# The output projection of a hybrid decoder layer as seven half products (Strassen's scheme) instead of eight

## The chip, the cores and the metric

The kernel runs on one core of one Trainium2 chip. The metric is device time in microseconds (us) of one execution. The engines are TensorE (PE; its weight loads are shown apart as PEld), VectorE (DVE), ScalarE (ACT), GpSimd (POOL) and SyncE (SP). SP issues nearly all DMAs here, in the order of its program, and each engine works through its own program in order and waits on semaphores.

## The reference

One layer on 1024 tokens of width 2048. A combined input projection feeds eight HGRN2 heads and four GLA heads, whose readouts are joined to y (1024 x 2048); then

```python
y = jnp.concatenate([y_h, y_g], axis=-1) @ w_out[i]
h = h + y.astype(dtype)

e = rms_norm(p[i] @ ple_proj[i], ple_norm_w[i])
gate = jax.nn.sigmoid(rms_norm(h, ple_gate_norm_w[i]) @ ple_gate_w[i] + ple_gate_b[i])
h = h + (gate * e).astype(dtype)
return rms_norm(h, final_norm_w)
```

The change is in the first of these lines, a product of a 2048 x 2048 weight matrix with the 2048 x 1024 matrix of y.

## The kernel before

All data is feature-major: a tile is 128 features by 512 tokens, and the 1024 tokens are two halves, h = 0 and h = 1. Every large product works with a split of both operands into a high part (rounded to fp32r) and a low part (the rest): three matmuls of 128 x 128 by 128 x 512 for each pair, low weight by high activation and so on (`passes`, L523 to L525). The activations of a stage lie in `act_hi` and `act_lo`, 16 tiles of 128 x 512 each. Writing them is a *fill*: `fill_high` on ACT (a cast to fp32r), then `fill_low` on DVE (source minus high part).

The weights come in *slabs*: 2048 x 128 of a weight matrix, 1 MB, as two halves `w_raw[0]`, `w_raw[1]` of 512 KB. For slab g SP loads the halves (`load_slab`, L371) as soon as the low halves of slab g-1 have been made; ACT casts them to `w_hi` when slab g-2 has been multiplied (`split_weights`, L778); DVE makes `w_lo` (`low_weights`, L1188). A slab takes 16 x 3 = 48 matmuls into one PSUM bank, `acc[0]` for even and `acc[1]` for odd slabs, and PE may start one only when the bank's last result has been taken out (`acc_free`).

The stages are, in order: the product of p (32 tiles), the input projection of half 0 (56 slabs) with the recurrences of its heads hung between the matmuls, the same for half 1, the output projection of half 0 and then of half 1 (16 slabs each), the gate projection of the two halves (16 slabs each), the final norm. The recurrence of a head is placed at fixed places between the matmuls of the next head's slabs (`hooks`): `k_transpose` and `state_update` in the first slab, seven levels (L588) in the second and third, `readout` and `o_transpose` later. The last head's hooks lie in the first slabs of the output projection.

In the output projection DVE takes a finished bank out (`h_begin`, L1565: h = acc + x, with the x tile loaded by SP into `xt_sb`), ACT squares it (L1047), DVE adds the square to a row sum (L1570). In the output projection of half 1, the tiles e of the p product, stored in HBM at the start, are loaded again, squared by ACT and summed by DVE. The readouts y of each head are stored to HBM (`y_scratch`, L380), and loaded before the stage that needs them (`load_y`, L384: four transfers of 1 MB). GpSimd does eight squares at the start of the kernel (L517) and nothing after it.

Of the kernel before, what the change touches and what calls it, by code (L numbers as in the profile page):

```python
# [38 lines left out]
P = 128  # L39
# [22 lines left out]
SLABS = E_SLABS + HALVES * (I_SLABS + 2 * KT)  # L62
# [7 lines left out]
def s_out(h):  # L70
    return E_SLABS + HALVES * I_SLABS + h * KT


def s_gate(h):
    return s_out(HALVES) + h * KT
# [67 lines left out]
def build(nc, x_feat, p, slabs, w_glr, w2, vec, lb_rows, masks, restart, ident_d, out, e_scratch, y_scratch):  # L143
    with ExitStack() as ctx:
# [91 lines left out]
        e_back = [unit(18), unit(21)]  # L236
        e_sqr = unit(20)
# [44 lines left out]
        ROWS_X, ROWS_H, ROWS_E, ROWS_F = (1, 2), (3, 6), (4, 5), (7, 8)  # L282
# [15 lines left out]
        act_free = sem("act_free")  # L298
        g_arg = sem("g_arg")
# [50 lines left out]
        def stage_end(a):  # L350

            return t_of((s_in, s_out, s_gate)[a // 2](a % 2 + 1) - 1)
# [8 lines left out]
        def _(sp):  # L361
            def load_slab(g, half=0):

                if isinstance(g, int):
                    stage = sum(g >= start for start in (s_in(1), s_out(0), s_out(1), s_gate(0), s_gate(1)))
                    at = g - (0, I_SLABS, I_SLABS, I_SLABS + KT, I_SLABS + KT, I_SLABS + 2 * KT)[stage]
                else:
                    at = g - half * I_SLABS
                for j in range(2):
                    sp.wait_ge(w_lo_ready, g * 2 + (j + 1))  # L370
                    sp.dma_start(w_raw[j][:, :], slabs[bass.ds(at, 1), j, :, :].rearrange("o p n -> (o p) n")  # L371
                                 ).then_inc(raw_loaded[j], 16)
# [10 lines left out]
            def load_y(h, q):  # L383
                sp.dma_start((feat, work)[h][:, 4 * q:4 * q + 4, :], y_scratch[h, 4 * q:4 * q + 4].rearrange("k p n -> p k n")  # L384
# [26 lines left out]
            for h in range(HALVES):  # L411
                base = s_in(h)
                if h:
# [4 lines left out]
                    sp.wait_ge(y_stored, h * Y_STORES * 16 + 16)  # L418
                    for q in range(4):
                        load_y(0, q)  # L420
# [3 lines left out]
                with sp.Fori(1, NH) as n:  # L424
                    for j in range(2, 6):
                        load_slab(n * SLABS_H + (base + j), h)
                    store_y(h, n + (h * HEADS - 1), n - 1, 1)
                for s in range(NH * SLABS_H + 2, NH * SLABS_H + 7):
                    load_slab(base + s)
# [1400 lines left out]
```

## Time and profile before

| | |
|---|---|
| median of 3 runs | 2258.35 us (2257.3 to 2260.07) |
| profiled execution, its own time | 2257.98 us |
| its span in the profile | 2255.9 us |
| PE busy | 2228.4 us, 99% of the span |
| PE weight loads, DVE, ACT, POOL busy | 82%, 65%, 44%, 0% |
| mean granted TensorE clock | 0.994 |

The time of the profiled execution is 2.1 us above its span, the start and end that the span does not hold. Busy times overlap between engines. A matmul's row shows its whole passage through the engine, so rows of PE overlap; the distance between starts is what one costs.

### The profile page before, as it was taken

To read this page: it belongs to the slowest core of one execution; us is meant where nothing else is said; L and a number is where in the kernel's file an instruction comes from. 1 tells how busy PE (TensorE), PEld (TensorE's weight loads), DVE (VectorE), ACT (ScalarE), POOL (GpSimd) and SP (SyncE) were. 2 spreads that over 40 slices of the span, in tenths; PEclk is the share of its full clock that TensorE was granted. 3 is DMA by queue.
4 is the path that set the end of the run, shared out by engine and by line. 5 is a ranking of instruction groups with operands and counts; after the bars stand their busy time and mean duration, and the time that the engine had idled before them with its cause. 6 is when DMAs were issued, how large, how long until landed. Compare 5 with 4: busy or idle time off the path is not lost.

```text
span 2255.9 us, 30769 instructions
## 1 busy us (share of the span) xinstructions
PE 2228.4 (99%) x10574; PEld 1857.8 (82%) x10574; DVE 1467.7 (65%) x2885; ACT 996.6 (44%) x1695; POOL 10.2 (0%) x12
## 2 busy tenths in 40 slices
PE   8999999999999999999999999999999999999996
PEld 7888888888888888888888888888888888887885
DVE  7567777775566666767666555566336448768875
ACT  6455544544333444444444333343224336446443
POOL 1000000000000000000000000000000000000000
PEclk9999999999999999999999999999999999999998
DMA  8622222222222224232222322222634553332442
GB/s 288 205 80 80 97 84 92 79 82 96 86 92 84 84 75 164 79 98 83 93 79 80 98 85 93 84 94 92 220 117 154 168 180 113 129 127 106 159 160 102
DMA packets 88438, 257.26 MB, mean 114 GB/s; under 512 B 9232, under 2 KB 9488, under 8 KB 88368
## 3 DMA queue, kind: packets, MB, share of 16 engines
q1 hardware_dynamic: 88368, 256.35, 33.9%
q8 instruction: 41, 0.67, 0.1%
q14 instruction: 29, 0.24, 0.0%
HBM read 231.15 MB, written 25.17 MB: 114 GB/s over the span
## 4 chain that ended last, share of the span: by engine, by line
PE 95%; DVE 2%; ACT 1%; DMA 1%; issue 0%; SPq 0%; DVEq 0%; ACTq 0%
PE acc L523 28%; PE acc L524 28%; PE acc L525 28%; PE lv L588 3%; PE so L597 1%; PE so L600 1%; PE so L577 1%; PE ms L566 1%; DMA w_raw<-in_slabs 1%; DVE sq_sum L1519 1%; DVE act_lo L1207 0%; PE tr L612 0%; PE tr L554 0%; PE tr L562 0%; PE ms L619 0%
## 5 line engine op out<-in xcount | busy, mean ns | idle before, releaser
L523 PE MATMUL acc<-act_hi,w_lo 128*128 128x512 f32 x2880 | 1154.5, 401 | 2.1 <-DVE act_lo L1207 1.4
L525 PE MATMUL acc<-act_hi,w_hi 128*128 128x512 f32 x2880 | 1124.1, 390 | 0.0
L524 PE MATMUL acc<-act_lo,w_hi 128*128 128x512 f32 x2880 | 1123.8, 390 | 0.0
L523 PEld LDWEIGHTS acc<-act_hi,w_lo 128*128 128x128 f32 x2880 | 542.4, 188 | 115.6 <-issue 9.7
L525 PEld LDWEIGHTS acc<-act_hi,w_hi 128*128 128x128 f32 x2880 | 541.1, 188 | 114.6
L524 PEld LDWEIGHTS acc<-act_lo,w_hi 128*128 128x128 f32 x2880 | 542.4, 188 | 104.6 <-issue 2.0
L778 ACT CAST w_hi<-w_raw 128x1024 fp32r<-128x1024 f32 x356 | 357.8, 1047 | 513.7 <-PE acc L525 477.2
L1188 DVE TENSOR_TENSOR w_lo<-w_raw,w_hi 128x1024 fp32r<-128x1024 f32 x356 | 420.3, 1220 | 81.6 <-ACT w_hi L778 81.4
L842 ACT ACTIVATE work<-work 128x512 f32<-128x512 f32 x120 | 75.6, 630 | 163.4 <-DVE work L1254 162.7
L792 ACT ACTIVATE work<-work 128x512 f32<-128x512 f32 x95 | 60.1, 632 | 140.2 <-DVE work L1234 140.2
L1268 DVE COPY_PREDICATED work<-mask_sb,lv 128x256 f32<-128x256 uint8 x168 | 88.6, 528 | 7.2
L588 PEld LDWEIGHTS lv<-work 128*128 128x128 f32 x480 | 71.9, 190 | 9.4
L1260 DVE TENSOR_TENSOR work<-work 128x256 f32<-128x256 f32 x120 | 50.9, 424 | 38.7 <-ACT work L842 38.7
L588 PE MATMUL lv<-work 128*128 128x128 f32 x480 | 72.6, 274 | 0.0
L786 ACT ACTIVATE work<-work 128x512 f32<-128x512 f32 x104 | 65.8, 633 | 3.3
L788 ACT ACTIVATE work<-work 128x512 f32<-128x512 f32 x104 | 65.8, 633 | 3.3
L1172 DVE MEMSET vec_dummy<- 128x1 f32 x209 | 12.3, 59 | 78.4 <-PE lv L588 74.8
L1053 ACT ACTIVATE work<-work 128x512 f32<-128x512 f32 x32 | 20.0, 624 | 87.7 <-DMA work<-e_scratch 85.6
L1565 DVE TENSOR_TENSOR feat<-acc,state_h 128x512 f32<-128x512 f32 (+1 forms) x16 | 11.0, 686 | 70.0 <-PE acc L525 64.2
L1239 DVE SCALAR_TENSOR_TENSOR work<-acc,work 128x512 f32<-128x512 f32 x48 | 33.2, 692 | 33.8 <-ACT work L792 33.8
L1254 DVE TENSOR_TENSOR work<-work 128x256 f32<-128x256 f32 x120 | 50.4, 420 | 0.0
L1253 DVE TENSOR_TENSOR work<-work 128x256 f32<-128x256 f32 x120 | 50.3, 420 | 0.0
(246 smaller groups left out, 1758.5 us busy)
## 6 DMA issues: line engine op xcount, KB each, us to landing
w_raw<-in_slabs SPq DMA_DIRECT2D x356, 512.0 KB, 4.1
work<-e_scratch SPq DMA_DIRECT2D x64, 256.0 KB, 4.6
feat<-in_x_feat SPq DMA_DIRECT2D x8, 1024.0 KB, 12.1
e_scratch<-work SPq DMA_DIRECT2D x32, 256.0 KB, 5.8
state_h<-in_x_feat SPq DMA_DIRECT2D x32, 256.0 KB, 2.6
y_scratch<-work SPq DMA_DIRECT2D x16, 256.0 KB, 2.0
y_scratch<-work SPq DMA_DIRECT2D x8, 512.0 KB, 2.8
feat<-y_scratch SPq DMA_DIRECT2D x4, 1024.0 KB, 9.2
```

The source lines that it names most:

```text
L523: nc.tensor.matmul(ps, lhs_lo, rhs_hi, start=start, stop=False)
L524: nc.tensor.matmul(ps, lhs_hi, rhs_lo, start=False, stop=False)
L525: return nc.tensor.matmul(ps, lhs_hi, rhs_hi, start=False, stop=stop)
L588: last = nc.tensor.matmul(scores[:, :, c * half:(c + 1) * half], x_lv[l % 3][:, c * C:(c + 1) * C], queries[:, :, c * half:(c + 1) * half] ...
L778: nc.scalar.copy(w_hi[par][:, j, :], w_raw[j][:, :]).then_inc(w_hi_ready, 1)
L786: st.mark(A(t1, t1, ACT.Exp, scale=-1.0))
L788: A(t1, t1, ACT.Ln, bias=1.0).then_inc(sp_ready, 1)
L792: A(t2, t2, ACT.Exp).then_inc(sig_ready, 1)
L842: A(x_lv[l % 3], x_lv[l % 3], ACT.Exp).then_inc(lv_exp, 1)
L1188: v.tensor_tensor(w_lo[par][:, j, :], w_raw[j][:, :], w_hi[par][:, j, :].bitcast(F32), ALU.subtract).then_inc(w_lo_ready, 1)
L1260: st.mark(v.tensor_tensor(keys, keys, lower_tokens(k_t, s), ALU.mult))
L1268: v.copy_predicated(upper_tokens(attn, s), mask_sb[:, l, :].rearrange("p (b n s) -> p b n s", b=2, s=s), lv_ps[l % 2][:, 0:TH // 2].rearra ...
```

## The change

y is cut into four blocks of 1024 features by 512 tokens, B11 and B21 of half 0, B12 and B22 of half 1, and w_out into four blocks of 1024 x 1024. The four blocks of the result are made from seven products of a 1024 x 1024 with a 1024 x 512 matrix, in place of eight. Four of the weight matrices are sums of blocks (in the order of the products P5, P6, P7, P3), three are blocks (P1, P2, P4); four of the activations are sums: T1 = B12 - B11, T3 = B22 - B12, T2 = T3 + B11, T4 = T2 - B21 (the signs are those of the code).

*Slabs.* An output slab now holds 8 x 128 weights for each of two tiles: its half j goes to `acc[j]` with 8 x 3 matmuls (`out_parts`). There are 28 slabs: n = 0 to 7 are P1 and P2 in turn, 8 to 15 P5 and P6 in turn, 16 to 19 P3, 20 to 27 P7 and P4 in turn. Both halves of the tokens are finished in one stage, and the gate stage follows.

*Sums of weights.* During the eight HGRN heads of half 1, SP loads each head 2 MB of blocks of w_out into `feat` (`load_blocks`), GpSimd makes four sums of 128 x 1024 (`block_sums`), and SP stores 2 MB to `w_sums` in HBM (`store_sums`).

*Sums of y.* T1 is made by GpSimd in `feat` after the HGRN heads of half 1 (4 MB loaded, 2 MB stored). T3, T2 and T4 are made by GpSimd during output slabs 5 to 11. The last head's y is stored in SP's place for n = 5, then come four loads of 1 MB, and in n = 6 the rows shown below.

*Fills.* Six fills of 8 tiles lie in the output projection (`FILLS_AT`), in the programs of ACT and DVE ahead of the taking out of that slab's banks: T1 at n = 7 for slab 8, T2 at 8 for slab 9, B22 at 15 for slab 16, T3 at 17 for slab 20, T4 at 20 for slab 21, the first half of the gate stage's at 27. T1 comes through four buffers of one tile; B22, T3 and T4 through three, each loaded again once `fill_low` has read it.

```diff
+def out_slab(n):
+    if n < 8:
+        return (P1, P2)[n % 2], n // 2
+    if n < 16:
+        return (P5, P6)[n % 2], (n - 8) // 2
+    if n < 20:
+        return P3, n - 16
+    return (P7, P4)[n % 2], (n - 20) // 2
...
+        FILLS_AT = {7: 10, 8: 11, 15: 12, 17: 13, 20: 14, OUT_SLABS - 1: 4}
...
+            for n in range(OUT_SLABS):
+                for j in range(2):
+                    if n in (2, 4, 6):
+                        load_x_tile(n + j)
+                    if 14 <= n < 18:
+                        load_x_tile(8 + 2 * (n - 14) + j)
+                    if 18 <= n < 26:
+                        load_x_tile(16 + 2 * (n - 18) + j)
...
+                if n == 7:
+                    for k in range(4, HK):
+                        load_t1(k)
...
+                for a, first, rest in ((12, 13, 15), (13, 16, 17), (14, 18, 20)):
+                    for k in range(HK):
+                        if n == (first if k < 3 else rest):
+                            load_t(a, k)
...
+                load_slab(S_OUT + n + 3)
...
+            def block_sums(c):
+                a11, a12, a21, a22 = (feat[:, 2 * u:2 * u + 2, :].rearrange("p k n -> p (k n)") for u in range(4))
+                pool.wait_ge(sum_loaded, c * 64 + 64)
+                g.tensor_tensor(a22, a21, a22, ALU.add).then_inc(sums_done, 1)
+                pool.wait_ge(sums_done, c * 4 + 1)
+                g.tensor_tensor(a21, a11, a21, ALU.subtract).then_inc(sums_done, 1)
...
+                for j in range(2):
+                    pe.wait_ge(acc_free[j], OUT_PAIR + n + 1)
+                    pe.wait_ge(w_hi_ready, g * 2 + (j + 1))
+                    pe.wait_ge(w_lo_ready, g * 2 + (j + 3))
+                    for k in range(HK):
...
+            for n in range(5, OUT_SLABS):
+                low_weights(S_OUT + n + 1, (n + 1) % 2)
+                if n == 21:
+                    row_factors(ROWS_E[0], r_e[0], e_sum[0])
+                if n == OUT_SLABS - 1:
+                    row_factors(ROWS_E[1], r_e[1], e_sum[1])
...
+                first = {5: 4, 7: 6}.get(n, 2 * n - 22 if 15 <= n < 27 else None)
+                if first is not None:
+                    for q in (first, first + 1):
+                        x_part(q)
+                if n in FILLS_AT:
+                    for k in range(HK):
+                        fill_low(FILLS_AT[n], k)
+                if n < OUT_SLABS - 1:
+                    for j in range(2):
+                        out_part(n, j)
+                        out_end(n, j)
+                        if 9 <= n < 25:
+                            e_add(2 * (n - 9) + j)
```

`x_part` adds the x tile, `out_part` adds a finished bank (P2, P3, P4: one addition; P6 and P7: two; P1 and P5 are copied out by ACT), `out_end` adds a square to the row sum. In the first output slabs, ACT and DVE do the last six tiles of y's fill later than before, and DVE takes out P2's first bank behind `next_level(R, 2)` and two `x_part`.

Three places show what stands in a row. The first is SP in the output projection at n = 6, from the loading of slab 8 (its first row) to that of slab 9: x tiles, four tiles of T1 (w2_sb, glr_t and two of work), three of B21, then twice a 1 MB load of B11 behind a wait for GpSimd and a 1 MB store of T3, then slab 9, and only then the last four tiles of T1.

```order
L472 DMA w_raw0<-w_sums 128x1024 [waits w_lo_ready]
L472 DMA w_raw1<-w_sums 128x1024 [waits w_lo_ready]
L563 DMA state_h<-in_x_feat 128x512 [waits xt_used] x2
...
L632 DMA work<-y_scratch 128x4x512 [waits t3_done]
L634 DMA t_sums<-work 128x4x512
L632 DMA work<-y_scratch 128x4x512 [waits t3_done]
L634 DMA t_sums<-work 128x4x512
L472 DMA w_raw0<-w_sums 128x1024 [waits w_lo_ready]
L472 DMA w_raw1<-w_sums 128x1024 [waits w_lo_ready]
L575 DMA w2_sb<-t_sums 128x512 [waits act_lo_ready]
L575 DMA glr_t<-t_sums 128x512 [waits act_lo_ready]
L575 DMA work<-t_sums 128x512 [waits act_lo_ready] x2
```

Before, the same engine had between two slabs of the output projection one x tile, and at one place the four loads of y of half 1.

```order
L371 DMA w_raw0<-in_slabs 128x1024 [waits w_lo_ready]
L371 DMA w_raw1<-in_slabs 128x1024 [waits w_lo_ready]
L384 DMA work<-y_scratch 128x4x512 [waits y_stored]
L384 DMA work<-y_scratch 128x4x512 x3
L443 DMA state_h<-in_x_feat 128x512 [waits acc_free1]
L371 DMA w_raw0<-in_slabs 128x1024 [waits w_lo_ready]
```

The second place is DVE in the output projection at n = 15: low weights of slab 16, two x parts, the eight tiles of B22's fill, and behind them the taking out of slab 15's banks (L1826).

```order
L1436 TENSOR_TENSOR w_lo<-w_raw,w_hi 128x1024 x2
L1816 TENSOR_TENSOR work<-work,state_h 128x512 x2
L1452 TENSOR_TENSOR act_lo<-work,act_hi 128x512 x8
L1826 TENSOR_TENSOR feat<-feat,acc 128x512
L1828 TENSOR_TENSOR work<-work,feat 128x512
L1850 TENSOR_TENSOR state_g<-state_g,work 128x512
```

Before, DVE had for a slab of the output projection of half 0 these rows, with the taking out first.

```order
L1565 TENSOR_TENSOR feat<-acc,state_h 128x512
L1188 TENSOR_TENSOR w_lo<-w_raw,w_hi 128x1024 x2
L1570 TENSOR_TENSOR sq_sum<-sq_sum,work 128x512
```

So the fill moved ahead of the release of a bank, and the same holds at n = 7, 17, 20 and 27. The third place is GpSimd in the HGRN heads of half 1, where nothing stood before:

```order
L699 TENSOR_TENSOR feat<-feat 128x1024 [waits sum_loaded]
L701 TENSOR_TENSOR feat<-feat 128x1024 [waits sums_done]
L703 TENSOR_TENSOR feat<-feat 128x1024 [waits sums_done]
L705 TENSOR_TENSOR feat<-feat 128x1024 [waits sums_done]
```

Each of the four waits for the one ahead; DVE's and PE's programs in these heads did not change.

## Rows read from the trace of the kernel before

**Rows 1.** The page, part 1: busy us, share of the span, instructions.
```profile
PE 2228.4 (99%) x10574; PEld 1857.8 (82%) x10574; DVE 1467.7 (65%) x2885; ACT 996.6 (44%) x1695; POOL 10.2 (0%) x12
```
**Rows 2.** Waits of PE: us in total, times, longest.
```profile
PE lv L636 <- DVE sq_sum L1519: 4.4, 1, 4.4
```
**Rows 3.** Timeline in the output projection: start us, us, engine line.
```profile
1680.33 0.39 PE L525 MATMUL acc<-act_hi,w_hi 128*128 128x512 f32 x1
...
1683.05 0.39 PE L525 MATMUL acc<-act_hi,w_hi 128*128 128x512 f32 x1
```
**Rows 4.** Timelines of DVE and ACT in the output projection of half 0.
```profile
1544.21 0.42 DVE L1254 TENSOR_TENSOR x_lv<-work 128x256 f32<-128x256 f32 x1
...
1556.04 2.01 ACT L778 CAST w_hi<-w_raw 128x1024 fp32r<-128x1024 f32 x2 [7.48 <-PE acc L525]
...
1604.00 2.00 ACT L778 CAST w_hi<-w_raw 128x1024 fp32r<-128x1024 f32 x2 [8.35 <-PE acc L525]
...
1605.08 2.36 DVE L1188 TENSOR_TENSOR w_lo<-w_raw,w_hi 128x1024 fp32r<-128x1024 f32 x2 [0.26 <-ACT w_hi L778]
...
1614.88 2.00 ACT L778 CAST w_hi<-w_raw 128x1024 fp32r<-128x1024 f32 x2 [8.35 <-PE acc L525]
```
**Rows 5.** Timeline of SP, then one row of ACT, around y's loads.
```profile
1587.09 0.43 SPq L380 DMA_DIRECT2D y_scratch<-work  x1
...
1606.34 1.47 SPq L371 DMA_DIRECT2D w_raw<-in_slabs  x2
1607.85 4.26 SPq L384 DMA_DIRECT2D work<-y_scratch  x4
...
1617.22 1.46 SPq L371 DMA_DIRECT2D w_raw<-in_slabs  x2
...
1626.19 1.05 ACT L778 CAST w_hi<-w_raw 128x1024 fp32r<-128x1024 f32 x1 [8.78 <-DMA w_raw<-in_slabs]
```
**Rows 6.** Windows: width, busy us of each engine, clock, DMA share, GB/s.
```profile
1619.00:1622.00 3.00, 3.00 (x15) 2.49 (x14) 0.00 (x0) 0.00 (x0) 0.00 (x0) 1.00 1.05 401
```
**Rows 7.** The page, part 6: DMA issues, KB each, us to landing.
```profile
state_h<-in_x_feat SPq DMA_DIRECT2D x32, 256.0 KB, 2.6
...
y_scratch<-work SPq DMA_DIRECT2D x8, 512.0 KB, 2.8
```
**Rows 8.** Timelines: a fill on DVE and ACT; row factors on DVE, first and last.
```profile
1512.73 4.90 DVE L1204 TENSOR_TENSOR act_lo<-feat,act_hi 128x512 fp32r<-128x512 f32 x8
...
1520.08 2.17 ACT L819 CAST act_hi<-feat 128x512 fp32r<-128x512 f32 x4
...
37.25 0.69 DVE L1194 TENSOR_SCALAR lv<-lv 128x512 f32<-128x512 f32 x1
...
41.58 0.69 DVE L1182 TENSOR_TENSOR work<-work,sq_sum 128x512 f32<-128x512 f32 x1
```
**Rows 9.** Windows around PE's one long wait, and its first row after.
```profile
34.00:35.00 1.00, 1.00 (x4) 0.81 (x3) 0.00 (x0) 0.46 (x1) 0.00 (x0) 0.50 0.00 0
35.00:36.00 1.00, 1.00 (x4) 0.76 (x4) 0.00 (x0) 1.00 (x2) 0.00 (x0) 0.71 0.03 12
...
29.87 2.07 PE L636 MATMUL lv<-sq_sum,ones 128*128 128x512 f32 x2 [4.40 <-DVE sq_sum L1519]
```
**Rows 10.** GpSimd alone and beside DVE; DVE's durations min/median/max in that stretch.
```profile
14.18 1.04 POOL L517 TENSOR_TENSOR state_h<-feat 128x512 f32<-128x512 f32 x1 [0.67 <-DMA feat<-in_x_feat]
...
20.53 1.48 POOL L517 TENSOR_TENSOR state_h<-feat 128x512 f32<-128x512 f32 x1 [0.69 <-DVE sq_sum L1519]
...
L1519 DVE TENSOR_TENSOR sq_sum<-sq_sum,work x8: 691/805/1440, 12.6 to 26.2; 128x512 f32<-128x512 f32 x8
```
**Rows 11.** Timelines of one HGRN head of half 1: SP, DVE, PE.
```profile
1155.17 0.35 SPq L380 DMA_DIRECT2D y_scratch<-work  x1
...
1174.64 0.41 DVE L1261 TENSOR_TENSOR x_lv<-x_lv,work 128x256 f32<-128x256 f32 x1
...
1178.54 0.60 PE L588 MATMUL lv<-x_lv 128*128 128x128 f32 x4
```

More of the change, by code:

```diff
@@ L140, in fresh, with build @@
             self.n = 0
[L143 removed]
+def build(nc, x_feat, p, slabs, w_glr, w2, vec, lb_rows, masks, restart, ident_d, out, e_scratch, y_scratch, w_sums, t_sums):
     with ExitStack() as ctx:
@@ L435, in _ @@
                 for s in range(I_SLABS - 5, I_SLABS + 1):
+                    if h and s == I_SLABS - 5:
+                        sp.wait_ge(t1_done, HK)
+                        sp.dma_start(t_sums[0].rearrange("k p n -> p k n"), feat[:, 0:HK, :]).then_inc(t1_stored, 16)
+                    if h and s == I_SLABS - 3:
+                        sp.wait_ge(t1_stored, 16)
+                        for q in range(4):
+                            load_y(0, q)
                     load_slab(base + s)
@@ L706, in _ @@
             last_head = rec_hooks(R, 2, 1) + [{7: lambda: readout(R, 2, 1)}, {13: lambda: o_transpose(R, 2)}, {}]
-            def o_pair(h, i, hooks=({}, {}), fill=None, frees=False):
-                for par in range(2):
-                    g = s_out(h) + par
-                    slab(i * 2 + g, par, i + t_of(s_out(h)) // 2, hooks[par],
-                         fill=fill if par == 0 else None, frees=frees and par == 1)
             def g_pair(h, i, hooks=({}, {}), fill=None, frees=False):
@@ L1116, in _ @@
+            out_part(n, 0)
+            for k in range(HK, KT):
+                if k == KT - 2:
+                    split_weights(S_OUT + OUT_SLABS + 1, 1, (0,))
+                if k == KT - 1:
+                    out_part(n, 1)
+                fill_high(4, k)
+            split_weights(S_OUT + OUT_SLABS + 1, 1, (1,))
             st.fresh()
             def g_split(h, c, par):
-                split_weights(c + (s_gate(h) + 2), par)
+                split_weights(c + (s_gate(h) + 2), par, gate=True)
@@ L1592, in _ @@
+            next_level(R, 1)
+            next_level(R, 2)
+            for q in range(2):
+                x_part(q)
+            out_part(1, 0)
+            next_level(R, 3)
+            out_end(1, 0)
+            out_part(1, 1)
             next_level(R, 4)
-            o_low(0, 0, 1)
-            h_end(0, 0, 1)
+            low_weights(S_OUT + 3, 1)
+            out_end(1, 1)
             for l in (LEVELS - 2, LEVELS - 1):
                 mask_level(R, l)
-            h_begin(0, 1, 0)
-            o_low(0, 1, 0)
@@ L1651, in _ @@
-            e_add(31, e_sum[1])
             st.fresh()
```

621 lines of the change are left out of this document (395 added, 226 removed).

## The prediction

> **What bounds the kernel now.** I read the page's busy times first: PE is busy for 99% of the span, GpSimd for 10 us of it [rows 1]. The list of PE's waits comes next: its longest is 4.4 us, at the start of the kernel, and nothing in the output projection is in it [rows 2]. The timeline there has twelve matmuls between starts 2.72 us apart, so one costs 0.227 us [rows 3], and the ends of slabs seen from ACT's casts lie 10.88 us apart, which is 48 of them [rows 4]. So PE sets the time and never waits; a matmul removed gives all of its 0.227 us, and a wait added costs all of its length.
>
> **What is removed.** 32 output slabs of 48 matmuls become 28 of 48: 192 matmuls by 0.227 us are **43.5 us** less. That is the whole gain. The rest of the sum is waits that the change can bring. I write t for the time since PE began the slab spoken of.
>
> **B, the T1 fill at n = 7 (slab 8).** This is the largest term, and it is a matter of bytes. By rows 4, slab 7 begins at 1604.0 and slab 5 at 1582.2. DVE's low weights end 3.4 us after a slab's start (1607.4 against 1604.0), SP loads a slab then, so it reaches n = 5 at about 1587.1, where the store of the last y stands before too [rows 5]. It waits for it to land, 2.8 us [rows 7], and issues 4.2 MB of y at 1590.3. Then come, in SP's order: slab 8 (1.05 MB), nine tiles (2.36 MB), B11 and T3 in two pairs (4.2 MB), slab 9 (1.05 MB), and the last four tiles of T1 (1.05 MB). Together 13.9 MB. The queue moves at most 401 GB/s [rows 6]; with 390 GB/s that is 35.6 us, and with 1.6 us of latency the last tile of T1 is there at 1627.5. That the queue gives a late transfer no way past an earlier one is seen where y of half 1 is loaded now: a slab issued at 1617.2, behind 4.2 MB issued at 1607.9, is cast only at 1626.2, and ACT waited for it [rows 5]. ACT and DVE need 1.3 us more for the last tile (0.54 and 0.61 a tile, [rows 8]), DVE 0.7 to take out slab 7's first bank, which stands behind the fill. PE can go on at 1629.6; it has ended slab 7 at 1614.9. B is **14.7 us**. Were T1's tiles first in the queue it would be about 2 (below), so 2 to 17.
>
> **C, D, E, the fills at n = 15, 17, 20.** PE may not start the next slab until DVE has taken out this slab's first bank, and DVE does that behind the fill. Low weights of the next slab end at t = 5.0 (ACT first copies out P5's bank and squares an e tile), two x parts by 6.3, the first fill tile is read by 6.9. Only then may the fourth tile be loaded into its buffer; it is queued behind a slab and two x tiles and lands at 9.7 to 10.4 (2.6 us a tile, [rows 7]). It is cast and subtracted by 11.0; the seventh tile may be loaded then and lands at 13.7, the eighth at 14.3, and the eighth's fill ends at 15.5. The bank is out at 16.2, PE wanted it at 10.9: **5.3 us**. For D DVE first has a bank and a square of P3 to finish, 0.7 more: **6.0**. For E, P7's taking out is two additions, another 0.7: **6.7**. If the loads ran ahead, DVE alone would end at 6.3 + 4.9 + 0.7 = 11.9, a wait of 1.0. So 1 to 7 each.
>
> **F, G, the row factors.** At n = 21 the row factors of e, which take 5.0 us from first to last row [rows 8], lie between the low weights and the bank: DVE begins the slab 5.3 behind (second bank of P7, its square, e), low weights end at 8.1, factors at 12.9, two x parts at 14.2, bank at 14.9. PE wants it at 10.9, but runs this slab 2.5 us slower (below): **1.5**. At n = 27 the same factors come ahead of the eight tiles: 5.6 + 4.9 + 5.3 + 0.7 = 16.5, a wait of **5.6**; 3 to 7.
>
> **The clock.** PE's wait of 4.4 us at the start [rows 9] was followed by matmuls at granted clock 0.50, which is 1.2 of 2.4 GHz, until about 35.3, some 5.4 us after it went on at 29.87. Work of 5.4 us at half rate loses **2.7 us**. B, C, D, E and G are longer waits than that one, so each gets 2.7: 13.5. If the fall has come later after some, 0 to 17.
>
> **A, the first output slabs.** The bank of P2 that PE needs for slab 2 is taken out by DVE behind `next_level(R, 2)`. That ended at 1544.6 before [rows 4], and slab 2 began at 1543.7 (its end, 1556.04, less 10.88 and three levels of 0.5). The two x parts, 1.3 us, and the bank itself, 0.7, come on top. **3 us**, 0 to 5; too short for the clock.
>
> **I, GpSimd beside DVE in eight heads.** 2 MB of blocks go out behind the y store at 1155.2 [rows 11] and are there 7.4 us later. Four sums of 128 x 1024 follow; a sum of 512 took 1.04 us alone, 1.48 beside DVE, and DVE's addition of two SBUF tiles took 1.44 in place of 0.69 in that stretch [rows 10]. So GpSimd wants 8.3 us and takes about 11; DVE, whose additions run at half rate beside it, comes out some 4.5 late (an estimate: half of the time for which both work, less the gaps in DVE's own program). The result of DVE that PE needs next is ready at 1175.05 and used at 1178.54 [rows 11]: 3.5 us of cover. **1 us** in each of eight heads, **8 us**; with no overlap 0, with DVE wholly held up (8.3 - 3.5) 38. I take the low end since both engines went on in rows 10. The blocks' transfers, 5.4 us at 390 GB/s, start right behind the y store, while SP's next slab load waits for low weights; I take them as hidden, since a slab cast late by a few us has a whole slab's time of cover.
>
> The Trainium skill (GPSIMD Engine Reference, Specifications; Advanced Engine Details and Errata, VectorE Performance Modes) says that GpSimd and VectorE share an SBUF interface, and that the two interfere or block each other. By blocking alone the 38 us would be the sum; the durations above show sharing, so I keep that as a rival.
>
> **H, the T1 sums.** SP waits 2.8 us for a y store and puts 4.2 MB (10.8 us) ahead of a GLA slab, and GpSimd then works 8 to 12 us: **3 us**, 0 to 8. The loads of y of half 0 move to the last head and land before they are used.
>
> The sum: A 3, B 14.7, C to E 18, F and G 7.1, clock 13.5, H 3, I 8: 67.3. Less 43.5: +23.8 on the profiled execution's 2258.0 (span 2255.9 and 2.1 around it), which is 0.4 below the median. **2282 us.**
>
> **The rivals.**
> *R1, the waits in the output projection are mostly covered*: loads that I put behind each other overlap, the fills keep pace with PE, and only parts of B and G are left. Its point: if T1's eighth tile is in by 1618 and the three-buffer loads land in under 2 us, B is 5, C to E 1 each and short of the clock, G 3; with A 1, one clock loss and H and I at 4, it is 19 against 43.5: about 2234 us, faster. For it: my latencies are one after another and single misplacements add up. Against: the bytes of B are counted, and the bank stands behind the fill whatever the loads do.
> *R2, GpSimd blocks DVE*: 38 in place of 8, about 2312 us. For it, the doubled additions in rows 10; against, that GpSimd itself grew only from 1.04 to 1.48.
> *R3, gain and waits cancel*: B as said, C to E 2 each without the clock loss, about 2258.
>
> **How the numbers follow.** Forecast (2262 to 2302) 0.60, R1 (2216 to 2253) 0.26, R2 and beyond 0.07, R3 0.07. A measurement of this kernel tells 0.2%, 4.5 us, from no change. Faster 0.28, same 0.05, slower 0.67. The range leaves out R2 and the lower part of R1: 2236 to 2304.
>
> **What would show it.** PE's waits should list a wait of some 15 us ahead of slab 8, put down to DVE or ACT with the load of `w2_sb`, `glr_t` or `work` from `t_sums` behind it, and 5 to 7 us ahead of slabs 16, 18, 21 and the first gate slab, each with a granted clock of 0.50 behind it; PE's matmul rows for one slab stay 10.88 us. In the HGRN heads of half 1 against those of half 0, DVE's additions of two SBUF tiles should show means over 0.69 and a stage longer by about 1 us a head. The prediction is wrong if T1's last tiles land before 1618, if the queue moves more than 401 GB/s, if PE goes on without a bank's release that I count, or if the heads' stage is unchanged or longer by more than 3 us a head.

## The result, and the profile after

The changed kernel takes 2313.84 us (median of 4 runs, 2310.1 to 2316.28) against 2257.87 us (4 runs) on the same chip: a ratio of **1.0246**, 95% interval 1.0234 to 1.0258, 56 us slower. The direction was forecast, the size was not: 2282 with an upper bound of 2304. The profiled execution has a span of 2312.1 us, 56.2 more than before. Executions of this kernel differ by up to 6 us, those of the kernel before by 3.

The page's busy times, and the longest of PE's waits (us in total, times, longest):

```profile
PE 2205.8 (95%) x10382; PEld 1831.4 (79%) x10382; DVE 1572.9 (68%) x2978; ACT 1015.5 (44%) x1749; POOL 135.7 (6%) x76
...
PE acc L729 <- DVE feat L1837: 30.1, 4, 21.5
PE lv L819 <- DVE x_lv L1509: 17.8, 8, 2.2
PE acc L729 <- DVE work L1837: 16.6, 2, 8.6
PE acc L729 <- DVE feat L1826: 8.5, 1, 8.5
PE so L808 <- ACT work L1086: 6.7, 2, 5.6
```

The 192 matmuls are gone (10,574 in [rows 1], 10,382 now), and PE, which waited nowhere for more than 4.4 us [rows 2], has 79.7 us of waits in these five rows alone. Three kinds are to be seen. The rows on `acc` are the output stage: the next slab waits for a bank that DVE empties late. The row on `lv` has eight waits of 2.2 us, one for each HGRN head of half 1. The row on `so` holds a wait of 5.6 us at the start of the GLA part of half 1; its other 1.1 us stand in half 0 and stood there before too.

The starts of the same products in both traces give what each stretch costs. The products of the last level of the first and of the last head, after:

```profile
882.55 0.60 PE L819 MATMUL lv<-x_lv 128*128 128x128 f32 x4
...
1264.21 0.60 PE L819 MATMUL lv<-x_lv 128*128 128x128 f32 x4
```

They started at 878.40 and 1239.7 before, so they are 4.2 us later in the first head and 24.5 in the last. Ahead of these heads the changed kernel was 0.6 us early, so the heads of half 1 cost 25.1. In the prediction's terms:

| term | forecast us | measured us | where it is read |
| --- | --- | --- | --- |
| gain | -43.5 | -43.5 | 192 matmuls fewer, a slab's pace unchanged |
| A | 3 | 1.4 | wait at 1576.81 |
| B | 14.7 | 21.5 | before slab 8, 1669.64 |
| C, D, E | 5.3, 6.0, 6.7 | 8.5, 8.6, 8.0 | before slabs 16, 18, 21 |
| F, G | 1.5, 5.6 | 1.8, 5.5 | before slab 22 and the first gate slab |
| clock | 13.5 | 12.7 | the output stage's excess, less its waits |
| H | 3 | 7.3 | wait of 5.6 before 1326.39, and what follows |
| I | 8 | 25.1 | shift over eight heads |

The measured terms come to 100.3 - 43.5 = 56.8, against 56.2 in the spans; the 0.6 between them is the early start of the heads. That the sum closes is no test of it, since the clock term is what is left over in the output stage. Counted directly, the granted clock was 0.50 for 23.1 us of PE's work behind the five long waits, which is worth 11.6. The forecast terms come to 67.3. Of the 33 us between the two sums **17.1 are I, 7.1 are C to E, 6.8 are B, 4.3 are H**; A and the clock give 2.4 back.

**Where I comes from.** One head's four sums on GpSimd, then what DVE does in that time (start us, us), then PE's wait:

```profile
1184.10 2.70 POOL L699 TENSOR_TENSOR feat<-feat 128x1024 f32<-128x1024 f32 x1 [43.99 <-DMA feat<-in_slabs]
1186.88 2.44 POOL L701 TENSOR_TENSOR feat<-feat 128x1024 f32<-128x1024 f32 x1
...
1191.95 2.48 POOL L705 TENSOR_TENSOR feat<-feat 128x1024 f32<-128x1024 f32 x1
...
1184.45 0.68 DVE L1482 SCALAR_TENSOR_TENSOR work<-acc,work 128x512 f32<-128x512 f32 x1
1185.83 0.69 DVE L1487 SCALAR_TENSOR_TENSOR work<-acc,work 128x512 f32<-128x512 f32 x1 [0.70 <-ACT work L1013]
...
1187.01 2.60 DVE L1502 TENSOR_TENSOR work<-work 128x256 f32<-128x256 f32 x1
1190.31 1.85 DVE L1508 TENSOR_TENSOR work<-work 128x256 f32<-128x256 f32 x1 [0.70 <-ACT work L1082]
1192.08 2.63 DVE L1509 TENSOR_TENSOR work<-work 128x256 f32<-128x256 f32 x1
...
1200.46 0.71 PE L819 MATMUL lv<-x_lv 128*128 128x128 f32 x4 [2.22 <-DVE x_lv L1509]
```

The additions take 0.42 us without GpSimd (L1501 and L1502 in the same head, at 1194.63 and 1194.97: 0.41). Here three take 2.60, 1.85 and 2.63: each ends 0.3 us behind the end of one of GpSimd's sums. That is no half rate. DVE stands until the running instruction of GpSimd is over, gets one of its own through, and stands again. L1482 and L1487, which read `acc` in PSUM, keep their 0.68 and 0.69. The traces of the changed kernel and of all its variants say the same. In the fourteen together, 256 instructions of DVE begin and end within one of GpSimd's of 0.6 us or more; of these 241 read PSUM and 14 are MEMSETs, which read nothing. The single one with all inputs in SBUF began within 0.01 us of GpSimd's. It is not the kind of instruction either: T4's sums leave the addition `feat<-feat,acc` (L1826, 128x512) at its 0.69 us, while its neighbour L1828, all in SBUF, takes 1.36 and 1.84 in place of 0.69.

The three additions lose 5.8 us in the chain, and the cover of 3.5 that the prediction counted leaves the wait of 2.2 that PE shows. A head is longer by 2.7 us (short gaps of PE around the same products make up the rest), and by 1.6 more in two of the eight, where the clock fell behind the wait. Windows behind the wait of the fourth and of the seventh head, with the clock as the third value from the end:

```profile
1035.80:1037.00 1.20, 1.13 (x5) 1.13 (x6) 1.15 (x5) 0.48 (x1) 0.00 (x0) 0.50 0.82 222
...
1200.40:1202.00 1.60, 1.54 (x9) 1.37 (x10) 1.55 (x6) 0.63 (x1) 0.00 (x0) 1.00 0.97 205
```

So a wait of 2.2 us was sometimes followed by a fall of the clock and mostly not.

**Where B's and C's sizes come from.** SP around y's store and the loads behind it, ACT's cast of the late T1 tile, and the bank that PE waits for:

```profile
1618.81 1.46 SPq L472 DMA_DIRECT2D w_raw<-in_slabs  x2
1620.32 0.43 SPq L480 DMA_DIRECT2D y_scratch<-work  x1
1627.38 2.86 SPq L623 DMA_DIRECT2D work<-y_scratch  x4
...
1649.48 2.57 SPq L472 DMA_DIRECT2D w_raw<-w_sums  x2
1652.10 1.28 SPq L575 DMA_DIRECT2D w_sb<-t_sums  x1
...
1663.88 0.62 ACT L1059 CAST act_hi<-w_sb 128x512 fp32r<-128x512 f32 x1 [15.32 <-DMA w_sb<-t_sums]
...
1669.64 0.79 PE L729 MATMUL acc<-act_hi,w_lo 128*128 128x512 f32 x1 [21.47 <-DVE feat L1837]
```

The order is the one that I counted. What I undercounted is the landing of the last y: it is issued right behind the 1 MB of slab 7, and takes 1627.38 - 1620.32 = 7.1 us until SP goes on, where I took 2.8 from [rows 7]. That median is of eight stores, and the very store in question was one of them. It stood behind a slab in the kernel before too, and the list of DMA issues of that trace from 1583 to 1590 has it at 6.6 us:

```profile
y_scratch<-work SPq DMA_DIRECT2D x1, 512.0 KB, 6.6
```

The tiles of C to E repeat it on a smaller scale. In the fill at n = 15 the fourth tile is issued behind a slab and two x tiles, and ACT waits for it:

```profile
1754.81 8.04 SPq L584 DMA_DIRECT2D work<-y_scratch  x5
...
1760.21 0.62 ACT L1059 CAST act_hi<-work 128x512 fp32r<-128x512 f32 x1 [7.11 <-DMA work<-y_scratch]
```

It is there 5.4 us after its issue, where I took 2.6; the seventh and the eighth, with the queue nearly free, take 2.6 and 2.9.

The windows at slab 8 (width, busy of PE, PEld, DVE, ACT, POOL, then clock, DMA share, GB/s) show the queue full ahead of it and the price in clock behind it:

```profile
1655.00:1660.00 5.00, 0.00 (x0) 0.00 (x0) 0.00 (x0) 0.00 (x0) 4.35 (x5) 0.50 1.06 410
1669.60:1672.00 2.40, 2.36 (x6) 1.88 (x7) 1.38 (x2) 0.90 (x2) 0.00 (x0) 0.50 0.00 0
1672.00:1675.00 3.00, 3.00 (x11) 2.35 (x10) 2.07 (x4) 2.83 (x5) 0.00 (x0) 0.66 0.00 0
```

A granted clock of 0.50 is 1.2 of 2.4 GHz; 1.0 is back at 1674, 4.4 us after PE went on. Behind the other four long waits of the output stage it took 3.1 to 6.0 us, against 5.4 in [rows 9].

### The profile page after: what moved, and what is told of

Read it like the earlier page. It is cut to its first block, busy times and chain, and to the rows that moved or that the text cites. A ratio compares the mean times of both kernels' runs of the same rounds, so it can differ in the third digit from the quotient of the medians.

```text
span 2312.1 us, 30663 instructions
## 1 busy us (share of the span) xinstructions
PE 2205.8 (95%) x10382; PEld 1831.4 (79%) x10382; DVE 1572.9 (68%) x2978; ACT 1015.5 (44%) x1749; POOL 135.7 (6%) x76
## 4 chain that ended last, share of the span: by engine, by line
PE 79%; DVE 10%; ACT 4%; DMA 3%; issue 3%; POOL 1%; SPq 0%; DVEq 0%; ACTq 0%; POOLq 0%
PE acc L729 23%; PE acc L730 23%; PE acc L731 23%; PE lv L819 3%; DVE w_lo L1436 2%; PE so L828 1%; PE so L831 1%; DVE work L1509 1%; ACT w_hi L999 1%; DVE work L1502 1%; PE so L808 1%; DVE act_lo L1452 1%; DMA work<-y_scratch 1%; DMA w_raw<-in_slabs 1%; DVE act_lo L1455 1%
## 5 line engine op out<-in xcount | busy, mean ns | idle before, releaser
L729 PE MATMUL acc<-act_hi,w_lo 128*128 128x512 f32 x2816 | 1136.3, 404 | 57.1 <-DVE feat L1837 30.1
L730 PE MATMUL acc<-act_lo,w_hi 128*128 128x512 f32 x2816 | 1103.4, 392 | 0.0
L731 PE MATMUL acc<-act_hi,w_hi 128*128 128x512 f32 x2816 | 1103.3, 392 | 0.0
L729 PEld LDWEIGHTS acc<-act_hi,w_lo 128*128 128x128 f32 x2816 | 533.8, 190 | 171.7 <-DVE feat L1837 31.9
L731 PEld LDWEIGHTS acc<-act_hi,w_hi 128*128 128x128 f32 x2816 | 532.2, 189 | 113.7
L730 PEld LDWEIGHTS acc<-act_lo,w_hi 128*128 128x128 f32 x2816 | 534.2, 190 | 103.3 <-issue 2.0
L999 ACT CAST w_hi<-w_raw 128x1024 fp32r<-128x1024 f32 x348 | 350.1, 1047 | 390.4 <-PE acc L731 355.8
L1082 ACT ACTIVATE work<-work 128x512 f32<-128x512 f32 x120 | 75.6, 630 | 199.2 <-DVE work L1502 198.3
L1013 ACT ACTIVATE work<-work 128x512 f32<-128x512 f32 x95 | 60.1, 632 | 142.6 <-DVE work L1482 142.6
L1508 DVE TENSOR_TENSOR work<-work 128x256 f32<-128x256 f32 x120 | 63.0, 525 | 49.5 <-ACT work L1082 49.5
L699 POOL TENSOR_TENSOR feat<-feat 128x1024 f32<-128x1024 f32 x8 | 21.2, 2656 | 1142.3 <-DMA feat<-in_slabs 1142.3
L1509 DVE TENSOR_TENSOR work<-work 128x256 f32<-128x256 f32 x120 | 68.8, 574 | 0.0
L1502 DVE TENSOR_TENSOR work<-work 128x256 f32<-128x256 f32 x120 | 67.6, 563 | 0.0
L1009 ACT ACTIVATE work<-work 128x512 f32<-128x512 f32 x104 | 65.8, 633 | 3.3
L1007 ACT ACTIVATE work<-work 128x512 f32<-128x512 f32 x104 | 65.8, 632 | 3.3
L1487 DVE SCALAR_TENSOR_TENSOR work<-acc,work 128x512 f32<-128x512 f32 x48 | 33.2, 691 | 33.8 <-ACT work L1013 33.8
L1501 DVE TENSOR_TENSOR work<-work 128x256 f32<-128x256 f32 x120 | 53.4, 445 | 0.0
L1420 DVE MEMSET vec_dummy<- 128x1 f32 x230 | 13.6, 59 | 56.8 <-PE lv L819 51.7
```

Source lines behind the costliest of these rows:

```text
L729: nc.tensor.matmul(ps, lhs_lo, rhs_hi, start=start, stop=False)
L730: nc.tensor.matmul(ps, lhs_hi, rhs_lo, start=False, stop=False)
L731: return nc.tensor.matmul(ps, lhs_hi, rhs_hi, start=False, stop=stop)
L999: nc.scalar.copy(w_hi[par][:, j, :], w_raw[j][:, :]).then_inc(w_hi_ready, 1)
L1007: st.mark(A(t1, t1, ACT.Exp, scale=-1.0))
L1009: A(t1, t1, ACT.Ln, bias=1.0).then_inc(sp_ready, 1)
```

## The experiments

Thirteen kernels, each beside the kernel before on the same chip (medians 2256.98 to 2257.85 us). Those without an interval are one execution each. The changed kernel is 2313.84, and its own four executions lie between 2310.1 and 2316.3, so a single time that is 2 or 5 us off says little; there the reading rests on PE's waits in the trace.

### Term I: GpSimd beside DVE

**e1, sums of 8 columns.**
```diff
-(feat[:, 2*u:2*u+2, :].rearrange("p k n -> p (k n)") for u in range(4))
+(feat[:, 2*u:2*u+2, :].rearrange("p k n -> p (k n)")[:, 0:8] for u in range(4))
```


> The four GpSimd sums of each HGRN head of half 1 work on 8 columns in place of 1024, so most of the sums of weights are left out; all loads and stores of blocks stay. Theory A (a GpSimd instruction holds the SBUF interface that it shares with DVE, and that is what makes these heads longer): PE's wait of 2.23 us ahead of the third level is gone in all heads, a head takes 51.7 us again in place of 54.4, and the whole comes out some 25 us shorter, about 2288. Theory B (the 4 MB of block transfers a head delay slabs or stores): no change, 2312.

Measured: 2289.03 us, 25 less, as theory A had it. The transfers, semaphores and order are those of the changed kernel; only most of the sums are left out, and the eight waits on `lv` are gone. The heads of half 1 cost no time at all over the kernel before. So I is GpSimd's work, and all of its 25.1 us.

**e2, the same sums in instructions of 512 columns.**
```diff
+for w in range(2):
+    at = slice(512 * w, 512 * (w + 1))
+    g.tensor_tensor(dst[:, at], x[:, at], y[:, at], op).then_inc(sums_done, 1)
```


> The same sums, each of 1024 columns done as two instructions of 512. Theory A (held for the length of one instruction; a DVE addition of two SBUF tiles waits for the end of the one that runs): the wait that a DVE addition can meet halves, from up to 2.4 to up to 1.25 us, DVE loses some 3 us a head in place of 6, and 3.5 us of cover hide nearly all of it: about 2290. Theory C (the two engines share the interface by rate, in proportion to the elements): the same 6 us are lost, 2312.

Measured: 2312.0 us, no gain. DVE's rows of one head (GpSimd works from 1180.12 to 1191.81):

```profile
1182.72 0.78 DVE L1501 TENSOR_TENSOR work<-work 128x256 f32<-128x256 f32 x1
1183.42 1.51 DVE L1502 TENSOR_TENSOR work<-work 128x256 f32<-128x256 f32 x1
...
1186.28 1.52 DVE L1509 TENSOR_TENSOR work<-work 128x256 f32<-128x256 f32 x1
1187.72 1.50 DVE L1501 TENSOR_TENSOR x_lv<-work 128x256 f32<-128x256 f32 x1
1189.15 1.52 DVE L1502 TENSOR_TENSOR x_lv<-work 128x256 f32<-128x256 f32 x1
1190.59 1.31 DVE L1530 COPY work<-state_h 128x128 f32 x1
```

Theory A had the mechanism and the wrong time: it forecast 2290. The time is that of theory C, but its mechanism, a sharing by rate, is not what the rows show. Each stop is now 1.5 us in place of 2.6, the length of the shorter sum, and there are more of them, so that DVE's rows of a head lose the same 6 us. The two engines take turns, so DVE loses GpSimd's own time however it is cut.

**e3, the blocks' transfers cut to 8 columns**, with GpSimd adding full tiles of what stands in `feat`, and P5, P6, P7, P3 reading unsummed blocks.
```diff
-sp.dma_start(feat[:, 2*u:2*u+2, :], at.rearrange("p (k n) -> p k n", k=2))
+sp.dma_start(feat[:, 2*u, 0:8], at[:, 0:8])
```


> The block loads and stores in the HGRN heads of half 1 move 8 columns in place of 1024, and the output slabs that would read the sums read blocks of w_out, so the result of the projection is left out; GpSimd's instructions stay. Theory A: the heads stay at about 54.4 us, 2312. Theory B (transfers): the heads go back to 51.7 us, about 2288.

Measured: 2346.99 us, 33 slower than the changed kernel. No theory had this. The sums no longer wait for 2 MB and begin some 3 us after the first of the blocks' loads is issued, earlier in the head. The eight heads cost 57 us in place of 25. What they meet there, and the row of PE's waits for it, about 5 us in each head:

```profile
1203.71 2.90 DVE L1524 TENSOR_TENSOR work<-work 128x512 f32<-128x512 f32 x1
1206.53 2.59 DVE L1501 TENSOR_TENSOR work<-work 128x256 f32<-128x256 f32 x1
1209.05 2.60 DVE L1502 TENSOR_TENSOR work<-work 128x256 f32<-128x256 f32 x1
1212.36 1.84 DVE L1508 TENSOR_TENSOR work<-work 128x256 f32<-128x256 f32 x1 [0.70 <-ACT work L1082]
...
PE so L808 <- ACT work L1086: 46.7, 10, 5.6
```

Four stops in one unbroken chain towards PE. So the transfers are not the cost, and the place in the head matters: the next three runs move the sums on purpose.

**e7 and e8, the blocks loaded behind slab 4 or behind slab 3 of a head.**
```diff
 for j in range(2, 6):
     load_slab(n * SLABS_H + (base + j), h)
+    if h and j == 4:      # e8: j == 3, block n - 1, stores behind slab 5
+        load_blocks(n)    # stores at the start of the next head
```


> The changed kernel, with the loads of the four weight blocks moved from the start of a head (ahead of its slab 2) to behind its slab 4, and the stores of the sums to the start of the next head. GpSimd then adds about 36 us later in the head, beside the end of one head and the start of the next. Theory P (it depends on which DVE instructions the sums meet: only additions of two SBUF tiles stop, and only a stop in a chain that PE waits for costs): fewer such additions stand there (about half), the wait before the third level shrinks from 2.2 us, and of the 25 us of the eight heads 12 to 20 go: 2294 to 2302. Rival Q (DVE loses GpSimd's 10 us anywhere, and is never far from the path): no change, 2310 to 2316. The run without the transfers, 33 us slower with the sums at another place of the head, speaks for P.

> The changed kernel, with the loads of the four weight blocks moved to behind slab 3 of a head and the stores behind its slab 5, so that GpSimd adds while the levels of the recurrence run, one after the other, each with four additions of two SBUF tiles on DVE between PE's products. Theory P (place decides): each of the ten microseconds falls into the chain level by level, where DVE has some 1.3 us of waiting per level: the eight heads lose 20 to 45 us, 2308 to 2335. Rival Q (any place costs the same): 2310 to 2316. A time under 2300 would fell both.

Measured: e7 2349.83 us, e8 2341.66. For e7 I had expected a gain and it lost 36, and e8 came out 7 us above the range of theory P: the heads cost 61 and 50 us. Theory P is right that the place decides, and my reading of the place was wrong. I had counted additions of two SBUF tiles. DVE in e7, beside sums from 1196.91 to 1206.65:

```profile
1199.84 1.96 DVE L1423 TENSOR_TENSOR small<-small 128x4 f32<-128x4 f32 x1 [0.51 <-ACT small L1104]
1202.03 2.22 DVE L1427 TENSOR_SCALAR small<-small 128x4 f32<-128x4 f32 x1
1204.48 2.84 DVE L1562 TENSOR_SCALAR work<-work,small 128x128 f32<-128x128 f32 x4
...
1207.38 1.12 PE L842 MATMUL tr<-ident,work 128*128 128x128 f32 x4 [4.55 <-DVE work L1562]
```

Instructions on 4 columns that take 0.16 us stand for 2 us, TENSOR_SCALAR among them. The short additions between the rows shown (L1425, L1429) keep their 0.16: they slip through behind a stopped one before the next sum begins, so a turn can hold more than one instruction of DVE. A chain of small ones is the worst place, and the changed kernel's own place is the best of the four tried.

**e10, each sum apart.** Its waits and its double buffer in short:
```diff
+def after_slab(g):
+    pool.wait_ge(w_lo_ready, g * 2 + 4)
 for i, (dst, x, y, op) in enumerate(sums):
+    after_slab(s_in(1) + (c + 1) * SLABS_H + 2 + i)
     g.tensor_tensor(dst, x, y, op).then_inc(sums_done, 1)
```


> The changed kernel, with the same 32 sums of weights but not in a row of four: each of a head's four waits until DVE has made the low parts of another of the head's slabs (2, 3, 4, 5), and the eight sums of T1 wait in the same way for eight slabs of the GLA part; the blocks use both halves of feat in turn, so that the loads and stores have a head's time. GpSimd's work is unchanged. Theory S (DVE has some 6 us of reserve towards PE in a head: of the 10 us that four sums in a row take, 6 to 7 were absorbed and 3 came out, so single sums of 2.5 us, apart, fit inside it): the heads lose 0 to 8 us in place of 25 and T1's sums 0 to 3 in place of 7.3; 2288 to 2300. Rival Q (the reserve is used up over the head as a whole, or at these places there is none, as at the three other places tried, which lost 50 to 60): 2314 to 2350.

Measured: 2288.26 us, 25.6 less, at the lower end of theory S. Two of GpSimd's four sums of one head, each released by DVE's low weights (L1445 here), and DVE beside the second:

```profile
1113.59 2.42 POOL L717 TENSOR_TENSOR feat<-feat 128x1024 f32<-128x1024 f32 x1 [15.55 <-DVE w_lo L1445]
1122.60 2.39 POOL L717 TENSOR_TENSOR feat<-feat 128x1024 f32<-128x1024 f32 x1 [6.59 <-DVE w_lo L1445]
...
1123.02 2.25 DVE L1517 TENSOR_TENSOR x_lv<-x_lv,work 128x256 f32<-128x256 f32 x1
```

DVE still stops (the last row: 2.25 us for 0.42), but once at a time, and PE's eight waits are gone. The same 10 us of work cost 3.1 us a head in a row; apart, the eight heads together are 0.7 us longer. I read this so, that DVE has a few us of reserve towards PE and has it again after each slab. The run changed the place of the sums as well as their spacing, since each now begins where DVE has just ended a slab's low weights; no run parted the two.

### Terms B to G: the order of the output stage

**e4, the bank emptied inside the fill.** ACT and DVE take the finished slab's first bank before the fourth tile of the fill (the fifth at n = 7), and the last row factors move behind the fill.
```diff
+EARLY = {7: 4, 15: 3, 17: 3, 20: 3, OUT_SLABS - 1: 3}
 for k in range(HK) if n in FILLS_AT else ():
+    if k == EARLY.get(n):
+        part(0)
     fill_low(FILLS_AT[n], k)
```


> At n = 7, 15, 17, 20 and 27 DVE takes the slab's first bank out in the middle of the fill (behind 4 tiles at n = 7, behind 3 at the others) in place of behind its last tile, and the second row factors of e move behind the gate stage's first fill. If PE waits for the bank's release, as read from the trace: the waits of 8.5, 8.6, 8.0 and 5.5 us ahead of slabs 16, 18, 21 and the gate stage shrink below 1 to 2 us each, and the half-rate stretches behind them are gone: 25 to 38 us less, about 2280; slab 8's wait of 21.5 stays within 3, since it is for T1's last tiles. If PE waits for the filled tiles themselves: the same waits stand a few matmuls later, at slabs 16 and 21 at least, and only slab 18's goes (its fill is not for it): about 2300.

Measured: 2291.78 us, 22 less, between the 2280 and the 2300 of the two theories. C, D, E and G shrink from 8.5, 8.6, 8.0 and 5.5 us to 2.2, 4.4, 2.6 and 1.8. F, the row factors at n = 21, grows from 1.8 to 5.7. B, which I had expected to stay as it is, becomes two waits that are 8.3 us shorter together:

```profile
1651.59 0.79 PE L731 MATMUL acc<-act_hi,w_lo 128*128 128x512 f32 x1 [3.81 <-DVE feat L1839]
1665.37 0.76 PE L731 MATMUL acc<-act_hi,w_lo 128*128 128x512 f32 x1 [9.33 <-DVE act_lo L1454]
```

PE can do slab 8 in part while the T1 fill goes on. What is left there, 9.3 us, is the late tiles. The wait behind the fill, which the prediction named for each of these slabs, is shown by this run; an exchange of a few instructions gives 22 us of it back.

**e9, the last y stored ahead of slab 7. e5, T1's tiles 4 to 7 issued ahead of B11's loads and T3's stores.**
```diff
+if n == 4:                    # e9
+    store_y(1, HALVES * HEADS - 1, 2 * (NG - 1) + NH, 2)
 load_slab(S_OUT + n + 3)
...
 if n == 7:                    # e5: from n == 6 to here
+    for k in range(4, HK):
+        load_t1(k)
     for q in range(2):
         sp.wait_ge(t3_done, 4 * q + 4)
```


> The changed kernel, with the store of the last y issued ahead of slab 7 of the output stage in place of behind it. Theory S (the chain store, load, T3, B11, T2 sets the end of wait B, and the store's landing of 7.1 us stood in it for 4.3 us more than I took): B falls from 21.5 to 16 to 18 us, 2308 to 2310. Rival L (the last T1 tiles are late only because their buffers and the issue queue are, or the transfers fill the DMA engines up to 1660 in any order): B stays at 20 to 22 us, 2312 to 2315.

> The changed kernel, with T1's tiles 4 to 7 issued ahead of the loads of B11 and the stores of T3 instead of behind them and behind slab 9. Theory L (the order on SP's queue: T1's last tiles are issued 10 us late behind waits for T3's sums): the T1 fill ends 8 to 12 us sooner, and B falls to 10 to 13 us; T2's sums come 3 to 6 us later and may open a wait of up to 5 us before slab 9: 2302 to 2308. Rival V (volume: some 15 MB pass at 400 GB/s until then whatever the order, so that the wait only moves to slab 9): 2311 to 2315.

Measured: e9 2311.15 us, which lies within the changed kernel's own spread. The trace tells more: the store lands in 2.8 us now, and PE's wait before slab 8 is 16.7 in place of 21.5, so the landing of the y store was worth the 4.3 us that the prediction had missed. The total fell by less, 2.7, because e9 came to the output stage 2.4 us later: its granted clock had fallen in three heads in place of two, and for longer at the start of the GLA part. e5 2308.57: 9.2 us before slab 8 and a new wait of 5.5 before slab 9, where ACT may copy the bank of slab 8 out only behind the later sums of T2 and the first of T4. Both theories of e5 are half right: the order held T1 up, and half of the wait moves one slab on.

**e11, e4, e5 and e9 together.**

> The changed kernel, with the output stage's order alone changed: the bank of the slab before is emptied inside each fill (as in the run with -22 us), T1's tiles 4 to 7 are issued ahead of B11 and T3's stores (-5.2 alone), and the last y's store ahead of slab 7 (-2.7 alone). Theory O (the waits at slabs 8 and 9 are one chain of tile loads and of an emptied bank that comes too late): the parts mostly add up, 2282 to 2286. Rival V (the transfers from 1627 to 1660 fill the queues, so that what is left of the wait stands before slab 9 whatever the order): 2288 to 2292.

Measured: 2289.32 us, hardly less than e4 alone, as rival V had it: there is one wait of 12.2 us before slab 9, where ACT empties the bank of slab 8 only when the first of T4's sums is done. T2's sums, which stand ahead of it on GpSimd, began late because they waited for B11.

### Term H: the loads in front of a slab

**e13, T1's input in four pieces.**
```diff
+for j in range(1, 7):
+    load_slab(m * SLABS_G + (base + NH * SLABS_H + j), h)
+    for half in range(2) if m == 1 and j <= 4 else ():
+        sp.dma_start(...)     # tiles 2(j-1) and 2(j-1)+1 of each operand
```


> The changed kernel, with T1's input tiles (4 MB) loaded in four pieces of 1 MB, each behind one of four slabs of the GLA part, in place of all at once ahead of a slab; the sums of T1 stay in a row, as the tiles come. Theory T (term H is the slab behind the 4 MB: its cast waits 8.2 us for the load, 10 us of transfers at 400 GB/s): the wait of 5.6 us before the levels goes, and 5 to 7 us of the time: 2307 to 2309. Rival G (it is GpSimd's T1 sums beside DVE): the wait stays or comes later in another place: 2312 to 2316.

Measured: 2307.58 us, 6.3 less. The wait of 5.6 us is gone (PE's list has 1.1 us on `so`, as before the change), and the GLA part starts without any further delay: H is 0 in place of 7.3. But the pieces also part GpSimd's eight sums into four pairs, so this run doesn't tell the load from the sums. e10 does: its 4.2 MB stand ahead of the same slab, and its first T1 sum begins 7 us after PE's wait there. The cast of that slab waits for the load in both, and DVE's low weights and PE's wait behind it differ. First the changed kernel, then e10:

```profile
1314.65 1.05 ACT L999 CAST w_hi<-w_raw 128x1024 fp32r<-128x1024 f32 x1 [6.18 <-DMA w_raw<-in_slabs]
1320.11 4.50 DVE L1436 TENSOR_TENSOR w_lo<-w_raw,w_hi 128x1024 fp32r<-128x1024 f32 x2
...
1296.11 2.35 DVE L1445 TENSOR_TENSOR w_lo<-w_raw,w_hi 128x1024 fp32r<-128x1024 f32 x2
1300.26 2.93 PE L817 MATMUL so<-work 128*128 128x256 f32 x6 [2.75 <-ACT work L1095]
```

With the load alone PE waits 2.75 us, and the GLA part is 4.5 us later with the fall of the clock behind it. The other 2.8 us of H go with GpSimd's sums beside these low weights. In e13 the slab at this place is cast without waiting for a transfer.

### All together

**e12, e10 and e11 in one kernel; e14, with three more edits** (T1's pieces, B11's loads as each half of T3 is there, the first row factors of e at slab 24; the expectation below says "of x" for them).
```diff
+for q in range(2):
+    if n == 6 + q:
+        sp.wait_ge(t3_done, 4 * q + 4)
+        sp.dma_start(work[:, HK + 4*q:HK + 4*q + 4, :], y_scratch[0, 4*q:4*q + 4]...)
-if n == 21:
+if n == 24:
     row_factors(ROWS_E[0], r_e[0], e_sum[0])
```


> Both of the edits before: the sums of weights and of T1 apart, and the output stage's new order. Theory A+O (the loss of the change is these two things): the parts add up, so with 2288 to 2300 and 2282 to 2286 for the two alone it takes 2256 to 2272, about the kernel before. Against: if spreading the sums fails, 2282 to 2320.

> The kernel with the sums apart and the new order of the output stage (2265.0), with three more edits: T1's input in pieces, B11's two loads issued as soon as each half of T3 is there (ahead of T1's tiles 4 to 7), and the row factors of x (first half) taken at slab 24 in place of slab 21. Theory: T1's pieces give 3 to 5 us, B11's tiles come 5 to 8 us sooner and T2 and T4 with them, so that the wait of 12.5 us before slab 9 falls to 2 to 6; the 5.7 us before slab 22 fall to 1 to 3 or come back at slab 24: 2246 to 2258. Rival (T2 and T4 are 16 sums at 1.3 to 1.8 us beside DVE's low parts, and these set slab 9 whatever the loads): 2257 to 2262.

Measured: e12 2265.03 us (median of 9), ratio to the kernel before 1.0028, interval 1.0018 to 1.0038. The parts add up: 2313.8 - 25.6 - 24.5 = 2263.7. **e14 2250.51 us** (median of 6, 2247.62 to 2252.88) beside 2257.74 for the kernel before, ratio **0.9969**, interval 0.9957 to 0.9981: 0.3% shorter, a small gain but one clear of the noise. Its longest waits of PE:

```profile
PE acc L750 <- DVE work L1858: 6.5, 2, 4.4
PE acc L750 <- DVE act_lo L1473: 6.3, 5, 1.8
PE acc L750 <- ACT act_hi L1080: 5.6, 1, 5.6
```

The wait before slab 9 fell from 12.5 us (e12) to 1.7, with a new one of 5.6 before slab 8. That fits B11's late loads having held T2 and T4 up, but the three edits were not run apart. Of Strassen's 43.5 us, 7 are left as a gain in the best kernel so far.

## Why the prediction was right in direction and wrong in size

**The gain and the places were right.** The matmul's 0.227 us held, PE waits before slabs 8, 16, 18, 21 and the first gate slab as said, with a granted clock of 0.50 behind, and the clock term was 12.7 against 13.5. A, F and G are within 2 us. R1 and R3 fell: no wait was hidden, and the output stage by itself lost 67.9 us against the 43.5 that it saved. Two of the prediction's own signs of being wrong came: the heads are longer by 3.1 us each, and the queue moved 410 GB/s, though that is no cause of the miss.

**Term I was the step that failed: "DVE, whose additions run at half rate beside it, comes out some 4.5 late".** In rows 10 a sum of GpSimd took 1.48 in place of 1.04 and an addition of DVE 1.44 in place of 0.69, and I read that as two engines sharing a path. With both instructions about as long, taking turns and half rate look the same there. With GpSimd's instruction nearly six times as long as DVE's (2.44 us beside 0.42) the two readings differ. e1 shows that GpSimd's sums are the cause, and the rows of the changed kernel and of e2 show turns. Measured are 10.1 us of GpSimd, of which DVE's chain lost some 6, since some of DVE's instructions in that time read PSUM and some of it was idle; less the cover of 3.5 that is near the 2.7 by which a head is longer, 3.1 with the clock.

The prediction's rival R2 had this mechanism and was given 0.07. It took GpSimd's 8.3 us in full, less 3.5 of cover, 4.8 a head or 38. That its total of 2312 lies within 2 us of the measured time is luck: its I is 13 us too large, and its other terms are 16 too small.

The Trainium skill (GPSIMD Engine Reference, Specifications) gives GpSimd's SBUF interfaces as shared with VectorE, with contention for VectorE's instructions in a 2-port perf mode or with two SBUF inputs. These rows agree: additions with two SBUF inputs took up to 2.60 us for 0.42, and additions with one input in PSUM kept their time.

**Terms B to E: the landing times were mis-sized.** "It waits for it to land, 2.8 us" was 7.1, and "lands at 9.7 to 10.4 (2.6 us a tile)" was 5.4 us for the tile that stands behind a slab and two x tiles. I had applied the rule that the queue lets nothing pass to the bytes of B, from [rows 5], and not to the single small transfer behind 1 MB: nearly all transfers in the medians of [rows 7] had the queue to themselves. The store's own landing of 6.6 us stood in the trace before the change. e9 shows it for the store (4.7 us off the wait). For C to E it is read from the trace and was not tried alone.

**Term H** named both causes, "10.8 us ahead of a GLA slab" and the sums on GpSimd, and put 3 us where it is 7.3. e10 shows 4.5 for the load without the sums; the 2.8 that remain are term I's mistake again.

**What stays open:** the part of B that is not the store. DVE's fills beside GpSimd's sums (1.58 and 1.75 us in place of 0.68 in two tiles there) account for 2.0 of the 2.5 us by the rows, but no run separated them. Why one wait of 2.2 us was followed by a fall of the clock and the next was not, stays open as well; e9 shows that it is part of what makes one execution differ from another.

## What to carry to other kernels

An engine that has nothing to do is not free: its instruction can hold another engine for the whole of its length, so the price is up to its own busy time wherever the other has a chain towards the bound. Cutting the instruction did not help here; putting single instructions apart did, one behind each event after which the other engine has reserve again. Two readings that fit the same rows are told apart by instructions of unlike length, so look for such rows before giving a rival a small chance. A transfer's landing time is that of the place in its queue: before a median of the page is used, see what the new transfer stands behind. And where an engine fills buffers for the next stage, empty the bank that the next slab needs inside the fill, not behind it.

## What the runs showed of the hardware

- GpSimd's tensor_tensor (128x1024 f32, three operands in SBUF) takes 2.4 to 2.5 us, the first of a row up to 2.7. A DVE instruction with all inputs in SBUF that begins beside it ends with it or up to 0.3 us later, whatever its size: 128x4 in 1.96 us for 0.16, 128x256 in 2.60 for 0.42. The DVE instructions that read PSUM kept their time (128x512 in 0.68 and 0.69 us).
- The turns cost GpSimd little: 2.44 to 2.48 us beside DVE in a row, 2.39 to 2.42 apart.
- The same wait of 2.2 us left the granted clock at 1.0 in six heads and at 0.50 in two; all five waits of the output stage of 5.5 us or more had 0.50 behind them, for 3.1 to 6.0 us of PE's work.
- A store of 512 KB behind 1 MB of loads on the same queue landed after 7.0 us, 2.8 with the queue free (e9); a load of 256 KB behind a slab and two x tiles after 5.4, and 2.6 with the queue nearly free.
